# Keeping x in SBUF between the merge phase and the norm phase, summing its squares in the merge phase, and reordering the first loads

## The reference, cut to what matters

```python
def rmsnorm(x, w):
    xf = x.astype(jnp.float32)
    xf = xf * lax.rsqrt(jnp.mean(xf * xf, axis=-1, keepdims=True) + NORM_EPS)
    return (xf * w.astype(jnp.float32)).astype(x.dtype)

def trunk_layer(x, c, ...):
    mod = jax.nn.silu(c) @ ada_w + ada_b
    shift, scale, gate = jnp.split(mod[:, None, :], 3, axis=-1)
    h = rmsnorm(x, norm_w) * (1.0 + scale) + shift
    proj = h @ w_in
    ...                      # three token mixers: retention, forgetting attention, gated delta
    out = jnp.sum(br * mg, axis=2) @ w_out
    return x + gate * out, new_state
```

## Time and profile before

| | |
|---|---|
| median of 3 runs | 3080.16 us (3079.82 to 3083.72) |
| profiled execution, its own time | 3077.81 us |
| its span, first to last instruction | 3076.0 us |
| mean granted PE clock | 0.989 |
| PE busy | 2929.1 us, 95% of the span |
| DVE, ACT, POOL busy | 1134.9, 1012.8, 809.6 us |
| HBM read and written | 208.20 MB and 57.60 MB |

### The profile page before, as it was taken

One profiled execution on the slowest core, in us unless ns is written; L12 is line 12 of the kernel. 1 busy time (PEld: TensorE's weight loads), 2 busy tenths in 40 slices (PEclk: granted clock), 3 DMA queues, 4 the chain that ended last, 5 costly groups with the idle time before them and its releaser, 6 DMA issues. The chain is left out here.

```text
span 3076.0 us, 55523 instructions
## 1 busy us (share of the span) xinstructions
PE 2929.1 (95%) x24012; PEld 2676.0 (87%) x24012; DVE 1134.9 (37%) x2548; ACT 1012.8 (33%) x1820; POOL 809.6 (26%) x528
## 2 busy tenths in 40 slices
PE   6999999999999999999979999999999999999996
PEld 4989888888888898999968898888888898899995
DVE  3411234334534543255133213334353543532631
ACT  3221423323434544222041233323334544532201
POOL 1212222222323323332222222212223413333320
PEclk8999999999999999999989999999999999999998
DMA  6121233233212211253232112212211221223323
GB/s 230 58 76 37 99 113 118 92 112 116 59 51 57 61 48 57 94 182 103 88 121 70 67 49 92 93 51 78 85 46 57 61 68 37 75 84 144 131 95 145
DMA packets 109954, 269.37 MB, mean 88 GB/s; under 512 B 38992, under 2 KB 45264, under 8 KB 108688
## 3 DMA queue, kind: packets, MB, share of 16 engines
q1 hardware_dynamic: 109712, 265.83, 25.6%
HBM read 208.20 MB, written 57.60 MB: 86 GB/s over the span
## 5 line engine op out<-in xcount | busy, mean ns | idle before, releaser
L283 PE MATMUL ps<-sb_h_split,sb_w_split 128*128 128x364 f32 (+1 forms) x3264 | 1157.7, 355 | 8.1 <-POOL sb_w_split L340 4.2
L284 PE MATMUL ps<-sb_h_split,sb_w_split 128*128 128x364 f32 (+1 forms) x3264 | 1072.4, 329 | 1.4 <-issue 1.4
L285 PE MATMUL ps<-sb_h_split,sb_w_split 128*128 128x364 f32 (+1 forms) x3264 | 1072.5, 329 | 0.0
L283 PEld LDWEIGHTS ps<-sb_h_split,sb_w_split 128*128 128x128 f32 x3264 | 616.8, 189 | 67.4 <-issue 38.7
L284 PEld LDWEIGHTS ps<-sb_h_split,sb_w_split 128*128 128x128 f32 x3264 | 616.9, 189 | 7.3
L338 POOL CAST sb_w_split<-sb_w_raw 128x1024 fp32r<-128x1024 f32 x152 | 164.5, 1082 | 1742.7 <-PE ps L285 1454.3
L285 PEld LDWEIGHTS ps<-sb_h_split,sb_w_split 128*128 128x128 f32 x3264 | 614.2, 188 | 1.5 <-issue 1.5
L340 POOL TENSOR_TENSOR sb_w_split<-sb_w_raw,sb_w_split 128x1024 fp32r<-128x1024 f32 x152 | 367.3, 2417 | 12.2
L1392 DVE COPY sb_fox<-ps 128x512 f32<-128x512 f32 (+3 forms) x208 | 109.1, 542 | 283.2 <-PE ps L1265 282.7
L325 ACT ACTIVATE sb_raw_qk<-ps 128x364 f32<-128x364 f32 (+2 forms) x176 | 64.6, 394 | 332.7 <-PE ps L285 332.6
L1331 ACT ACTIVATE sb_fox<-sb_fox 128x128 f32<-128x128 f32 (+5 forms) x144 | 111.2, 772 | 114.0 <-DVE sb_fox L1370 113.8
(11 more groups left out here) (275 smaller groups left out, 4382.1 us busy)
## 6 DMA issues: line engine op xcount, KB each, us to landing
sb_w_raw<-in_wblk SPq DMA_DIRECT2D x154, 512.0 KB, 5.6
sb_ada_fox<-in_adaw SPq DMA_DIRECT2D x32, 512.0 KB, 4.3
sb_raw_qk<-scratch_gate SPq DMA_DIRECT2D x24, 544.0 KB, 3.6
sb_fox<-scratch_fcum SPq DMA_DIRECT2D x8, 1600.0 KB, 7.2
sb_w_raw<-in_wbr SPq DMA_DIRECT2D x48, 256.0 KB, 4.1
scratch_gate<-sb_fox SPq DMA_DIRECT2D x16, 544.0 KB, 7.8
scratch_gate<-sb_delta SPq DMA_DIRECT2D x16, 544.0 KB, 4.5
sb_h_split<-scratch_o SPq DMA_DIRECT2D x16, 544.0 KB, 10.4
```

Source lines behind the costliest of these rows:

```text
L283: pe.matmul(out, w_hi, x_hi, start=first, stop=False)
L284: pe.matmul(out, w_hi, x_lo, start=False, stop=False)
L285: return pe.matmul(out, w_lo, x_hi, start=False, stop=last)
```

## The change

Five things change.

1. The conditions are loaded first, into a buffer of their own (`c_raw`), with a semaphore of their own; `fixed_loaded` counts masks alone. `adab` and `dsmall` are loaded behind the first two parts of `adaw`, and DVE waits for them ahead of its first use.
2. One tensor (`sb_x`) holds mg and x of the merge phase and x of the norm phase behind it, with one more row `sums`. In the merge phase SP loads x in 4 DMAs of two rows over the rows of mg that have been split.
3. In the merge phase ACT squares row j when DVE has updated it, and DVE adds the square to `sums` (`add_square`), one row later than the update. Row 0 is squared into `sums` itself, so that there are 7 additions.
4. The norm phase behind it loads no x and squares nothing; PE makes 3 products of `ones` with `sums` in place of 24, after DVE has left the merge phase. ACT's Ln waits by segment.
5. The merge phase of layer 0 loads blocks 0 and 1 of layer 1, stores x to `dx` behind that, and doesn't wait for the stores; DVE waits for them (`x_kept`) ahead of scaling x in layer 1. The merge phase of layer 1 stores nothing.

```diff
@@ norm_phase, SP
                     if first_layer:
+                        sp.dma_start(c_raw[:, :, :], A["cT"]).then_inc(c_loaded, 16)
                         sp.dma_start(masks[:, :, :], A["masks"]).then_inc(fixed_loaded, 16)
-                    for c in range(4):
-                        sp.dma_start(x[:, 2 * c:2 * c + 2, :], src[2 * c:2 * c + 2].rearrange("k p t -> p k t"))\
+                    for c in range(4 if first_layer else 0):
+                        sp.dma_start(x[:, 2 * c:2 * c + 2, :], A["xT"][2 * c:2 * c + 2].rearrange("k p t -> p k t"))\
                             .then_inc(branch_loaded[c], 16)
-                    if first_layer:
-                        sp.wait_ge(fixed_set, 4)
-                        sp.dma_start(cT[:, :, 0:2], A["cT"]).then_inc(fixed_loaded, 16)
-                        sp.dma_start(adab[:, :, :], A["adabT"]).then_inc(fixed_loaded, 16)
-                        sp.dma_start(dsmall[:, :], A["dsmall"]).then_inc(fixed_loaded, 16)
...
                         for m in range(2):
                             load_ada(sp, m)
-                    load_block(sp, L, 0)
-                    load_block(sp, L, 1)
+                        sp.dma_start(adab[:, :, :], A["adabT"]).then_inc(small_loaded, 16)
+                        sp.dma_start(dsmall[:, :], A["dsmall"]).then_inc(small_loaded, 16)
                     if first_layer:
+                        load_block(sp, L, 0)
+                        load_block(sp, L, 1)
@@ norm_phase, PE
                     if first_layer:
-                        pe.wait_ge(fixed_loaded, 64)
-                    for k in range(KC):
-                        pe.wait_ge(squares, k + 1)
+                        pe.wait_ge(fixed_loaded, 16)
+                    if first_layer:
+                        ...                  # the 24 products as before
+                    else:
+                        pe.wait_ge(done["dve"], nr)
                         for s, (a, w) in enumerate(SEGS):
-                            mm = pe.matmul(ps[:, s, 0:w], ones, sq[:, k % 2, a:a + w],
-                                           start=(k == 0), stop=(k == KC - 1))
-                        mm.then_inc(squares_used, 1)
+                            pe.matmul(ps[:, s, 0:w], ones, sums[:, a:a + w], start=True, stop=True)\
+                                .then_inc(squares_used, 1)
@@ norm_phase, ACT
-                        act.wait_ge(fixed_loaded, 64)
-                        act.activation(cT[:, :, 0:2], cT[:, :, 0:2], ACT.Silu).then_inc(fixed_set, 1)
-                    for k in range(KC):
+                        act.wait_ge(c_loaded, 16)
+                        act.wait_ge(fixed_set, 4)
+                        act.activation(cT[:, :, 0:2], c_raw[:, :, :], ACT.Silu).then_inc(fixed_set, 1)
+                    for k in range(KC if first_layer else 0):
...
-                    act.wait_ge(squares_used, KC)
                     for s, (a, w) in enumerate(SEGS):
+                        act.wait_ge(squares_used, KC if first_layer else s + 1)
@@ norm_phase, DVE
                         dve.wait_ge(params_loaded, 48)
+                        dve.wait_ge(small_loaded, 32)
...
+                        dve.wait_ge(x_kept, 16 * KC)
                         normalise(0)
@@ merge, SP
-                    for j in range(KC):
-                        if j < NBLK - 10:
-                            await_split(sp, L, first + j + 6)
-                            load_block(sp, L, first + j + 10)
-                        sp.wait_ge(dve_took, 3 * (j + 1))
-                        sp.dma_start(dx[j], xbuf(j)).then_inc(x_stored[j % 3], 16)
-                        if j + 3 < KC:
-                            sp.wait_ge(x_stored[j % 3], 16 * (j // 3 + 1))
-                            load_x(j + 3)
-                    for i in range(3):
-                        sp.wait_ge(x_stored[i], 16 * len(range(i, KC, 3)))
+                    for j in range(NBLK - 10):
+                        if j == NBLK - 12:
+                            if L:
+                                sp.wait_ge(x_kept, 16 * KC)
+                            for c in range(4):
+                                sp.wait_ge(normed, 2 * c + 2)
+                                load_x(c)
+                        await_split(sp, L, first + j + 6)
+                        load_block(sp, L, first + j + 10)
+                    if L + 1 < DEPTH:
+                        await_split(sp, L, first + NBLK - 1)
+                        load_block(sp, L + 1, 0)
+                        load_block(sp, L + 1, 1)
+                        for j in range(KC):
+                            sp.wait_ge(dve_took, 3 * (j + 1))
+                            sp.dma_start(dx[j], mg[:, j, :]).then_inc(x_kept, 16)
@@ merge, ACT
+                    for j in range(KC):
+                        act.wait_ge(dve_took, 3 * (j + 1))
+                        if j >= 3:
+                            act.wait_ge(squares_used, j - 2)
+                        act.activation(squared(j), mg[:, j, :], ACT.Square).then_inc(squares, 1)
@@ merge, DVE
+                    def add_square(j):
+                        dve.wait_ge(squares, j + 1)
+                        if j >= 2:
+                            dve.wait_ge(squares_used, j - 1)
+                        dve.tensor_tensor(sums, sums, squared(j), ALU.add).then_inc(squares_used, 1)
...
                             ins.then_inc(dve_took, 1)
+                        if j >= 2:
+                            add_square(j - 1)
+                    add_square(KC - 1)
```

70 lines of the change are left out of this document (44 added, 26 removed).

## The result

| | before | changed |
|---|---|---|
| time, median (lowest to highest) | 3079.99 us (3077.88 to 3083.72), 4 runs | 3040.87 us (3040.10 to 3043.00), 4 runs |
| ratio, 95% interval | | 0.9873 (0.9856 to 0.9890) |
| profiled execution: time, span | 3077.81, 3076.0 us | 3043.00, 3041.1 us |

The change gains 39.1 us of the 49.7 that the prediction worked out. 3040.9 lies above its range of 3025 to 3039.

What follows compares the result with a forecast made beforehand. PE, busy 2929.1 of 3076.0 us, was taken as the bound, so only its 147 us of idleness could pay. Gains 8.5 + 20.2 + 21.0 = 49.7 off 3080.16 gave 3030.5 us, range 3025 to 3039.

Steps and rivals of the forecast that it cites:

- the step that weighed DVE against POOL: Merge phases: DVE's additions beside POOL's weight splits; POOL loses at most 1.3 us a split, far inside 8.5.
- POOL needs two times 1.0 + 2.4 us: Layer 0's start: POOL's time to split blocks 0 and 1, done by 35.5 us, wanted at 43.4.
- cover, 8 us and 1 us: Slack before PE would wait for splits: 8 us at the start, 1 us for block 2 at layer 1's border.
- The start, 8.5: Layer 0's first norm: earlier Squares bring PE's first projection product forward; gain 8.5 us, between 6.5 and 9.5.
- The border, 20.2: Layer 1's norm: DVE scales at T + 9.6 instead of T + 29.8 (T: DVE's last x update); gain 20.2 us.
- PE comes to its first product 4.5 us behind DVE's start: Layer 1's border: interval taken from the old trace, putting PE's first projection product at T + 14.1.
- The last norm, 21.0: End of kernel: DVE's idleness behind the last x update falls from 30.6 to 9.6 us; gain 21.0 us.
- The merge phases, 0: Merge phases: added Squares and additions fit into idle time and gaps; cost 0, bounds 0 and 1 us.
- The start gains nothing: Rival, start: the chain behind the squares hangs on the DMA queue; gain 41.2, time 3039 us; chance 0.08.
- A new wait takes half of the middle: Rival, layer 1's border: block 2's split or the x stores end 10 us later; 3040 us; chance 0.06.
- Slower: Rival, merge phases: DVE's additions delay POOL's splits, so PE waits each row; at 4 us, 3094; chance 0.02.
- the other rule that was weighed: Borders: a 1.38 us drain on top of each table load would make the total gain 2.8 us less.

Runs made afterwards that it cites:

- experiment 4: Changed kernel with weight blocks 0 and 1 of layer 0 loaded ahead of the modulation weights: 3037.7 us, ratio 0.9851.
- experiment 9: Changed kernel with the edits of experiment 4 and experiment 8, and layer 0's block 2 split held until the first convolution's rows are done: 3032.2 us, ratio 0.9837.
- experiment 11: The kernel of experiment 9 plus the wait of experiment 10: 3029.2 us, ratio 0.9828.
- experiment 8: Changed kernel with blocks 0 and 1 of layer 1 split in layer 0's merge phase into a kept buffer: 3040.0 us, ratio 0.9865.
- experiment 10: Changed kernel with POOL's splits in layer 1's first retention group held until q and k are turned: 3039.1 us, ratio 0.9859.
- experiment 5: Kernel before the change, with weight blocks 0 and 1 of layer 0 loaded ahead of the modulation weights: 3081.3 us, ratio 0.9995.
- experiment 2: Changed kernel with the old start: conditions and small constants loaded behind x, ACT waiting for all of them: 3047.3 us, ratio 0.9883.
- experiment 7: Changed kernel with the loads of blocks 3 to 6 of layer 1 held until four rows of h are ready: 3042.0 us, ratio 0.9872.

## Why the prediction was wrong

The sum was 8.5 + 20.2 + 21.0 with a cost of 0 elsewhere. What failed is the step that weighed DVE against POOL. It looked at it for the merge's additions alone, and asked there only whether POOL could be late. At the start and at the border it priced the splits by "POOL needs two times 1.0 + 2.4 us" and checked their cover, 8 us and 1 us, that is, whether *PE* would wait for them. That DVE's multiplications and scalings, which the change moves under those splits, would be held up themselves was never asked, although had an operation that doubled beside POOL. It cost 5.4 us at the start and 4.2 at the border's first product. The retention group of layer 1, which the sum doesn't have, took another 4.1 in the compared profiles.

*The start, 8.5.* First Square at 7.8, inside the bound of 7.9: right. Sums 17.67 us against 16.63, 1.0 where 0.5 was taken for the clock: inside its bounds. (Nine of PE's records there took 0.81 us or more ahead of the first of 0.47, five before.) Blocks 0 and 1 were split by 37.0 instead of 35.5: later than forecast, but covered, as said. Then the multiplications took 3.7 us more and the scalings of chunk 0 another 1.7; the first product came at 50.6, not 44. With the collision taken away it came at 44.8, 44.3 and 43.6 (experiments 4, 9 and 11). So the term was nearly right for a kernel without the collision: the gates' store of experiment 4 is 7.5 us ahead of that of before. The rest of the loss, 1.2 us up to the gates' store, goes with the lower clock in the second chunk; no run here takes that apart.

*The border, 20.2.* The sums began at T + 2.8, forecast as 2.9. DVE's start at T + 9.0 was forecast as 9.6, and lfc's arrival at T + 5.2 as about 7: better than worked out. POOL's times were right within a microsecond (block 2 begun at T + 11.7, done at T + 16.8, forecast T + 16). But "PE comes to its first product 4.5 us behind DVE's start" carried over the 4.5 us of a border at which POOL was already still. Here it was 9.3 us, and the border gained 15.7. With blocks 0 and 1 split elsewhere (experiment 8) the product is at T + 14.1. The chain that sets it is POOL's: in seven further profiles with these splits the product stands 15.53 to 15.55 us behind the sums' start, whether DVE started after 6.2 or after 7.1. Only where that chain is out of the way does the clock of the sums show at the product: 10.74 us behind their start where they took 2.07 (experiment 11), 11.59 where they took 3.96 (experiment 9).

*The last norm, 21.0.* Right: 21.5.

*The merge phases, 0.* Right: DVE still waits 3.38 us for PE ahead of its update, so PE sets the pace as before, although both operations got longer where they met: four of the seven additions took 1.58 us instead of 1.28, and four of POOL's six subtractions 3.33 instead of 2.40. From DVE's first update to T there are 92.3 us in either layer, 92.5 before. (The four banks of the prediction's argument are the four of the eight that this kernel gives to the output projection.)

*Not in the sum: the retention group of layer 1, -4.1.* It has no line in the diff, and the prediction didn't look there. In all twelve profiles with the new border DVE's products start 17.1 to 17.8 us behind the gates' store, against 16.1 and 16.7 in the two profiles of the old border, because `in_sret` lands later; what follows meets POOL's split. With the split held, PE's idle time ahead of its transposes is 3.0 and 2.9 us (experiments 10 and 11), against 4.7 and 5.3 with the old border; the stretch to the first state takes 81.6 and 83.2 us, against 83.2 and 84.6. A part of the 4.1 is spread between runs: up to the second state the two profiles of the old border need 200.6 and 202.0 us, the three of the changed kernel 204.7 to 206.4. The 1.3 us of the second group aren't a collision and no experiment took them away. Why the load lands later wasn't tried and stays open.

*Which rival came true?* None as written, though 3040.9 is near two of them. "The start gains nothing" came close to the number for the wrong reason: not what the DMA queue carries held the chain up, but that POOL's splits met DVE; another order of the loads pays only where it moves the splits away (experiments 4 and 5). "A new wait takes half of the middle" named POOL's block 2, but as something that PE waits for. The rival *Slower* had the right mechanism in the wrong phase and direction.

The Trainium skill (SBUF — State Buffer, SBUF: two separate sides) words the rule: whichever of the two starts first has the port pair for a whole instruction and "the other fully blocks", and an operation of VectorE with two SBUF inputs contends only with a GpSimd operation that reads SBUF. The prediction cited it and used half of it. The runs agree with all of it that they touch: DVE resumes to the hundredth where POOL's subtraction ends; with memsets in place of two subtractions the four scalings take 3.65 us; the DMA load makes no difference. Held too were, in experiment 2, operations with a single tensor as input, of which the words quoted here don't speak. Of the other rule that was weighed (ScalarE: Activation LUTs, What ACT_TABLE_LOAD costs: a drain of 1.38 us on every switch to another table set), nothing is seen at the new borders either: the load at 3024.33 takes 1.28 us and the Exp starts at 3025.62.

What stays open: some 4 us between runs of one and the same kernel in different groups. The profiles of the changed kernel's two repetitions are 5.8 us apart; 3.3 of these lie between the gates' store of layer 0 and T, 1.5 in the stretch from T to the gates' store of layer 1, and 1.5 in the two retention groups behind it. How much of it is the clock isn't shown: the granted clock in 1430 to 1460 us was 1.00 in both (0.89 to 0.94 in those of experiments 7 to 9), while the six records of sums behind T took 2.07 to 2.81 us in four profiles and 3.70 to 3.97 in the eight others. Nothing was run to steer this.

## What to carry to other kernels

When a change moves an operation of VectorE with two SBUF operands earlier, list what GpSimd does in that very stretch, and price the overlap in both directions: near the sum of both engines' times, not the longer one. (By estimate at the border here: 2.87 us of DVE and 5.7 of POOL make 8.6, and 7.82 were measured.) A saving ahead of such a meeting point can be given back there unless GpSimd's work moves as well: of 9.9 us at the start 3.0 arrived at the first product. Giving GpSimd its input earlier (experiments 4 and 5), or holding it for a few microseconds (experiment 10), cost nothing here. Look for operations whose duration doubles in the trace of before (smallest against largest of one line); each may be a collision that a shift of a few microseconds can worsen or mend.
